# Reordering the steps of the two middle blocks of a convolution and recurrence mixer: input preparation moved to their second part, key and router copies ahead of modulation

## The reference

```python
h = rms_norm(x, g_pre_mix[l]) * (1.0 + sc1) + sh1
proj = h @ w_in[l]
cv, cg, q, f, i, g = jnp.split(proj, IN_SPLITS, axis=-1)
y_conv = conv_module(cv, cg, dw_kernel[l], dw_bias[l], conv_ln_gain[l], conv_ln_bias[l])
y_rec = hgrn2(q, f, i, g, lb_table[l], rec_norm_gain[l])
y = jnp.concatenate([y_conv, y_rec], axis=-1) @ w_out[l]
x = x + gt1 * rms_norm(y, g_post_mix[l])
h = rms_norm(x, g_pre_ffn[l]) * (1.0 + sc2) + sh2
```

## Time and profile before

| | |
|---|---|
| median of three runs | 1663.68 us |
| the profiled execution | 1662.17 us, its span 1660.4 us |
| TensorE busy | 1520.1 us, 92% of the span, granted clock 0.954 on average |
| VectorE, ScalarE, GpSimd busy | 1210.6, 876.0, 367.1 us |
| steps of block 1 | 436.5 to 547.5 us |
| steps of block 2 | 678.0 to 787.4 us |

### The profile page before, as it was taken

How to read it: one execution, slowest core, us unless ns; L and a number is a source line. 1 busy time by engine, 2 the same in 40 slices (tenths; PEclk the granted TensorE clock), 3 DMA queues, 4 the chain that set the end, 5 groups by cost and what they waited for, 6 DMA issues and landing times. The chain is left out here.

```text
span 1660.4 us, 23932 instructions
## 1 busy us (share of the span) xinstructions
PE 1520.1 (92%) x7453; PEld 1106.6 (67%) x7455; DVE 1210.6 (73%) x1932; ACT 876.0 (53%) x1534; POOL 367.1 (22%) x396
## 2 busy tenths in 40 slices
PE   4899879999989999999999999658999999999974
PEld 2779754889755889666889565445676677766741
DVE  2587994597975598974698945576788878777837
ACT  3324362324574324563324533356788887878846
POOL 1000000000010000011000011123476667665640
PEclk8899979999999999999999998769999999999996
DMA  9452361332332323332321543469999998889859
GB/s 320 168 185 94 93 260 42 89 102 78 126 102 76 102 79 100 116 113 77 89 89 52 228 127 114 153 228 329 352 295 274 344 262 240 223 243 284 275 109 384
DMA packets 201445, 291.27 MB, mean 175 GB/s; under 512 B 10558, under 2 KB 158171, under 8 KB 201370
## 3 DMA queue, kind: packets, MB, share of 16 engines
q1 hardware_dynamic: 171840, 197.18, 34.8%
q0 software_dynamic: 29360, 92.99, 20.5%
q10 hardware_dynamic: 170, 0.10, 0.0%
HBM read 240.42 MB, written 59.26 MB: 180 GB/s over the span
## 5 line engine op out<-in xcount | busy, mean ns | idle before, releaser
L1038 DVE SCALAR_TENSOR_TENSOR cv<-late_rows,taps,cv 128x512 f32<-128x512 f32 x480 | 321.8, 746 | 0.0
L1962 DVE TENSOR_TENSOR w_rest<-wgu,w_high 128x1024 fp32r<-128x1024 f32 x192 | 233.8, 1221 | 88.9 <-ACT w_high L1885 85.5
L1885 ACT ACTIVATE w_high<-wgu 128x1024 fp32r x192 | 201.7, 1054 | 97.9 <-PE pgu L1830 75.9
L531 PE MATMUL bank<-wo,yT 128*128 128x512 f32 x512 | 226.5, 599 | 3.6 <-ACT hT L736 2.5
L488 PE MATMUL bank<-hT_high,tiles_operand 128*128 128x512 f32 x496 | 197.2, 398 | 1.1 <-DVE logits L1132 1.1
L489 PE MATMUL bank<-hT_operand,tiles_operand 128*128 128x512 f32 x496 | 196.6, 396 | 0.0
L490 PE MATMUL bank<-hT_high,win_operand 128*128 128x512 f32 x496 | 196.6, 396 | 0.0
L531 PEld LDWEIGHTS bank<-wo,yT 128*128 128x128 f32 x512 | 96.7, 192 | 119.7 <-issue 117.7
L1840 PE MATMUL py<-wd,hTe 128*128 x384 | 172.7, 592 | 1.8 <-DVE hTe L1985 0.9
L1828 PE MATMUL pgu<-w_high,x_high 128*128 128x512 f32 x384 | 156.8, 408 | 3.8 <-DVE x_rest L1977 3.8
L1016 DVE TENSOR_TENSOR win_operand<-win,tiles_operand 128x2048 fp32r<-128x2048 f32 x48 | 109.9, 2290 | 58.1 <-ACT tiles_operand L758 58.0
(11 more groups left out here) (389 smaller groups left out, 2846.7 us busy)
## 6 DMA issues: line engine op xcount, KB each, us to landing
win<-w_in_in SPq DMA_DIRECT2D x64, 512.0 KB, 5.2
wgu<-w_gate_in SPq DMA_DIRECT2D x32, 1024.0 KB
wgu<-w_up_in SPq DMA_DIRECT2D x32, 1024.0 KB
wd<-w_down_in SPq DMA_DIRECT2D x32, 1024.0 KB
win<-w_in_in SPq DMA_DIRECT2D x16, 1024.0 KB, 5.1
wo<-w_ada_in POOLq DMA_DIRECT2D x6, 2048.0 KB, 11.2
y_dram<-zeros POOLq DMA_DIRECT2D x17, 512.0 KB, 5.1
tiles<-x_in POOLq DMA_DIRECT2D x16, 512.0 KB, 6.0
```

What stands on the lines that cost most here:

```text
L531: last = nc.tensor.matmul(out[:], yT[:, w % 2, k, :], wo[:, k, half * 512:(half + 1) * 512], start=(k == 0), stop=(k == KD - 1))
L1038: ins = V.scalar_tensor_tensor(out=cv[:, j], in0=u[:, j, w:w + T], scalar=tap, in1=cv[:, j], op0=ALU.mult, op1=ALU.add)
L1885: A(w_high[:, QK * q:QK * q + QK, :], c.wgu[:, bass.ds(slot, 1), QK * q:QK * q + QK, :].rearrange("p a k n -> p (a k) n"), ACT.Copy).then_ ...
L1962: V.tensor_tensor(w_rest[:, part, :], c.wgu[:, bass.ds(slot, 1), part, :].rearrange("p a k n -> p (a k) n"), w_high[:, part, :].bitcast(F3 ...
```

## The change

The `MIDDLE` lists of TensorE, ScalarE and VectorE are written in a new order. Preparing the next block's input (`T`, `xsum`, `xnorm`, `raw`) leaves the first part of the steps: `T` 0 comes behind `O` 1, `T` 3 behind `B` 3. `y` 1 1 is cut in two halves of four matmuls, around `B` 0. On ScalarE `key`, `turned` of tile 1, `rin` of tile 0 and others stand where `high` and `raw` were; `gate` comes behind `x1sum` 0. On VectorE `scale` comes behind `mask` 0. At the end TensorE does `r` 2, `oT` 2, `r` 3 ahead of `l` 2 and `piece` 0. `T` of odd tiles takes banks 0 and 1. The square in `x_sums` writes its unused output to `hT` instead of `ob`, so `osave` of tiles 0 and 1 no longer waits for the next input's sums, and `modulate` waits for them.

```diff
@@ bank_of
-                return 2 * (1 if i == 3 else i) + half if t < 0 else 2 + half
+                return 2 * (1 if i == 3 else i) + half if t < 0 else 2 + half if t == 0 or i % 2 == 0 else half
@@ y_half
-            def y_half(t, w, half):
-                if half == 0:
+            def y_half(t, w, half, part=None):
+                first, final = part in (None, 0), part in (None, 1)
+                if half == 0 and first:
...
-                out = take("y", w, half, t)
-                for k in range(KD):
+                out = take("y", w, half, t) if first else place("y", w, half, t)
+                for k in range(0 if first else KD // 2, KD if final else KD // 2):
...
-                last.then_inc(y_ready, 1)
+                if final:
+                    last.then_inc(y_ready, 1)
@@ TensorE, MIDDLE
-            MIDDLE = [("y", 0, 0), ("T", 0), ("mean",), ("T", 1), ("y", 0, 1), ("T", 2), ("var",), ("T", 3), ("y", 1, 0),
+            MIDDLE = [("y", 0, 0), ("mean",), ("y", 0, 1), ("var",), ("y", 1, 0), ("A", 0), ("y", 1, 1, 0), ("B", 0),
...
@@ x_sums
-                if i == 0:
-                    wait(act, oT_psum, (t - 1) * NT)
-                ch.link(A(ob[:].rearrange("p a n -> p (a n)"), xt_of(t, i), ACT.Square, accum_out=sums[:, i:i + 1]))
+                ch.link(A(hT[:, :, i * P:(i + 1) * P], xt_of(t, i).rearrange("p (k n) -> p k n", k=KD), ACT.Square,
+                          accum_out=sums[:, i:i + 1]))
@@ modulate
+                dve.wait_ge(x_rstd, t * NT + i + 1)
@@ save_outputs
-                elif t < NB - 1:
-                    dve.wait_ge(x_rstd, (t + 2) * NT)
                 else:
-                    dve.wait_ge(oT_psum, t * NT)
+                    wait(dve, oT_psum, t * NT)
```

More of the change, by code:

```diff
@@ L915, in _ @@
                      ("turned", 3)]
[L916 to L923, removed]
+            MIDDLE = [("ln", 0), ("ln", 1), ("ln", 2), ("end", 0), ("exps", 0), ("sq", 0), ("sq", 1), ("sq", 2),
+                      ("sq", 3), ("exps", 1), ("end", 1), ("ln", 3), ("exps", 2), ("end", 2), ("var",), ("ysum", 0),
+                      ("exps", 3), ("end", 3), ("xsum", 0), ("key", 0), ("x1sum", 0), ("gate",), ("xsum", 1),
+                      ("ysum", 1), ("key", 1), ("rin", 0), ("osq", 0), ("orstd", 0), ("x1sum", 1), ("key", 2),
+                      ("raw", 0), ("turned", 0), ("osq", 1), ("rin", 1), ("raw", 1), ("orstd", 1), ("xsum", 2),
+                      ("turned", 1), ("high", 0), ("high", 1), ("split", 0), ("raw", 2), ("ysum", 2), ("x1sum", 2),
+                      ("osq", 2), ("xsum", 3), ("orstd", 2), ("high", 2), ("key", 3), ("ysum", 3), ("raw", 3),
+                      ("high", 3), ("x1sum", 3), ("rin", 2), ("osq", 3), ("rin", 3), ("orstd", 3), ("turned", 2),
+                      ("split", 1), ("turned", 3)]
             FINAL = [("ln", 0), ("ln", 1), ("ln", 2), ("end", 0), ("exps", 0), ("sq", 0), ("sq", 1), ("sq", 2), ("sq", 3),
@@ L1204, in _ @@
                      ("gateo", 2), ("oms", 3), ("gateo", 3), ("rest", 1), ("logit", 3)]
[L1205 to L1215, removed]
@@ new lines, in _ @@
+            MIDDLE = [("scan", 0), ("diff", 0), ("centre",), ("head", 0), ("scan", 1), ("diff", 1), ("scan", 2),
+                      ("head", 1), ("diff", 2), ("scan", 3), ("head", 2), ("diff", 3), ("head", 3), ("ynorm", 0),
+                      ("mask", 0), ("scale",), ("state", 0, 0), ("x1norm", 0), ("xnorm", 0), ("state", 0, 1),
+                      ("ynorm", 1), ("mask", 1), ("osave", 0), ("xnorm", 1), ("state", 1, 0), ("oms", 0),
+                      ("gateo", 0), ("place", 0), ("state", 1, 1), ("logit", 0), ("osave", 1), ("mask", 2),
+                      ("raw", 0), ("x1norm", 1), ("state", 2, 0), ("oms", 1), ("gateo", 1), ("raw", 1), ("place", 1),
+                      ("logit", 1), ("xnorm", 2), ("input", 0), ("state", 2, 1), ("osave", 2), ("raw", 2),
+                      ("input", 1), ("ynorm", 2), ("rest", 0), ("oms", 2), ("x1norm", 2), ("gateo", 2), ("input", 2),
+                      ("xnorm", 3), ("mask", 3), ("place", 2), ("state", 3, 0), ("raw", 3), ("ynorm", 3),
+                      ("osave", 3), ("state", 3, 1), ("input", 3), ("x1norm", 3), ("oms", 3), ("logit", 2),
+                      ("gateo", 3), ("logit", 3), ("place", 3), ("rest", 1)]
```

## The result

The changed kernel takes 1678.24 us (median of 4 runs, 1675.88 to 1680.62), the kernel before in the same comparison 1663.13 (4 runs, 1662.35 to 1665.45): a ratio of 1.0091, 95% interval 1.0075 to 1.0108. It is slower, as forecast, but by 15.1 us where 1671 meant 7.3, and 1678 lies outside the range of 1665 to 1677. The profiled execution, the slowest of the four, took 1680.62 us (span 1678.9) against 1662.17 (span 1660.4): 18.5 more.

A forecast was written before the change was run, and what follows sets the result against it. TensorE was taken to bound the middle blocks. Front -0.1 and end +3.8 make 3.7 us a block, 7.4 for two, on 1662.17: 1669.6, or 1671 as the runs' median; range 1665 to 1677.

The forecast's parts named there:

- The waits: Middle blocks: TensorE's new waits less those gone, front -0.1 and end +3.8, 3.7 us a block, 7.4 for two.
- The front comes out even: Up to y(2,0): gaps at y(1,0), B(0), O(0) gone, -3.65 us a block; new waits at O(1), B(2), +3.55.
- What was put at nothing: Middle blocks: later loads taken as 0 (0 to 1 us a block); square's new destination and lost output wait cost nothing.
- The clock: TensorE's granted clock in the middle blocks, as gaps go and come: from -1.6 us in all to +1.6 a block.
- rival 4: The clock falls in both middle blocks' new gaps: 1.6 to 3.2 us more, 1672 to 1675 by the runs; chance 0.15.
- Rival 3: Gate's two table loads each hold ScalarE 1.4 us longer, O(1) 2.8 later: 1675.2 (1677 by the runs); chance 0.03.
- Rivals 1 and 2: Middle blocks: gaps close without successors, 1656 by the runs, chance 0.05; or front gains, end still costs 3.8, 1663.5, 0.12.

The follow-up runs named there:

- E2: The changed kernel with dummy transposes in three TensorE gaps of each middle block, ahead of O(1), oT(2) and r(3): 1665.60 us, ratio 1.0023.
- E6: The kernel before, order untouched, with dummy transposes in some TensorE gaps of all four blocks: 1656.32 us, ratio 0.9968.
- E3: The changed kernel with ScalarE's sum of tile 1 and raw(0) and VectorE's xnorm(1) moved later at the middle blocks' front: 1673.62 us, ratio 1.0077.
- E5: The changed kernel with the old order at the middle blocks' end and the queue moves at their front together: 1660.64 us, ratio 0.9992.
- E4: The kernel before with only the order at the end of the middle blocks changed as in the change: 1673.86 us, ratio 1.0079.
- E1: The changed kernel with the old order at the middle blocks' end, T(3) kept ahead, ScalarE and VectorE queues reordered to suit: 1669.47 us, ratio 1.0037.

## Why the prediction was wrong in size

The ledger of the two middle blocks, from one execution each. E2 has the waits of the changed kernel with no fall of the clock, E6 those of the kernel before, also with none:

| | both blocks, us |
|---|---|
| before, no fall (E6) | 479.77 |
| waits: E2 less E6 | +7.03 |
| clock: after less E2 | +10.98 |
| clock: before less E6 | 1.59, to be taken off |
| after less before | 7.03 + 10.98 - 1.59 = 16.42 |

Block 2 of both, up to `y(2,0)` and over all steps, E2 first, then E6:

```profile
680.95:740.75 59.80, 56.38 (x295) 34.42 (x294) 45.78 (x88) 41.20 (x93) 6.61 (x10) 1.00 0.32 105
680.95:793.85 112.90, 108.31 (x563) 68.13 (x561) 74.94 (x147) 67.03 (x154) 11.08 (x16) 1.00 0.32 103
...
679.41:741.05 61.64, 57.86 (x308) 35.97 (x307) 50.89 (x101) 48.05 (x108) 6.62 (x10) 1.00 0.40 126
679.41:788.81 109.40, 104.97 (x533) 65.14 (x531) 74.72 (x147) 66.33 (x153) 11.10 (x16) 1.00 0.34 106
```

- **The waits: right.** Forecast 3.7 a block, 7.4 in all; measured 7.03. With the clock held up the steps take 112.90, where the forecast said about 113. Right in its parts too: gaps at y(1,0), B(0) and O(0) gone, A(0) on time, O(1), B(2), oT(2) and r(3) late by the amounts worked out.
- **"The front comes out even": right, for the waits.** At `y(2,0)` E2 is at 59.80, E6 at 61.64 with two more T (1.8) done by then: even within 0.1. The end then costs 3.5, forecast 3.8. O(1) starts 47.79 us into block 2, before 52.32 with four T (3.5) ahead of it: 1.0 ahead, forecast 0.9. E3 shows why: ysum(1) behind gate and sum of tile 1, and xnorm(1) ahead of the state update.
- **What was put at nothing** (loads, square, lost wait): right by E5.
- **The step that failed is "The clock".** The sum has nothing for it; as an unknown it was allowed from -1.6 in all to +1.6 a block, the size of block 1's surplus in the earlier trace rows, and rival 4 gave the fall in both blocks 0.15. It fell twice in each, and the term measures 9.4 net. The fall at the front was of the size allowed: up to `y(2,0)` the changed kernel needs 61.44 in block 2, 1.6 more than E2. The end is what was mis-sized, 4.0 there. The 1.6 of the earlier trace rows came from O(0)'s surroundings, a fall of some 3 us in work that half waits; at the end of the block TensorE was at 1.2 GHz from 788.5 to 798.5, through r(3), l(2) and the first matmuls of piece 0, 8.5 us busy in 10: E4 puts that at 4.1. The forecast had both gaps there in its sum, side by side, 3.85 us of them, and did not ask what they do to the clock and to the dense work behind.
- **Rival 4** was thus the mechanism, with a price (1.6 to 3.2) at most a third of the 9.4. **Rival 3** (dearer table loads) is out: the silu starts at 720.01, 0.01 behind the load's end at 720.00, and ScalarE passes through gate and loads in 5.5 us as before. **Rivals 1 and 2** are out by the timeline.
- The runs of one kernel spread by some 10 us, the slower ones at a lower mean clock (E1: 1669.97 at 0.948, 1660.51 at 0.958). That this is also why medians and block sums differ is likely, but not shown.

## What to carry to other kernels

Price a gap of TensorE twice: its idle time, and, where the clock falls, half the busy time that follows at the lower clock (half of 8.5 is 4.3; E4 has 4.1). Gaps of 1 to 2.5 us that stand close together, ahead of dense work, cost more by the second than by the first where it fell (4.1 against 3.0 at the end of this block). When an order is moved, keep the long unit (a y half, a projection piece) between a chain's start and its waiter; if a wait can't be covered, harmless matmuls into a free bank keep the clock up: E2's median is 2.7 above the kernel before, the changed kernel's 15.1.

## What the hardware showed that was not expected

- The granted clock falls with TensorE working most of the time: in E3 it fell in block 1 right behind three gaps of 0.75, 0.78 and 0.87 us, the longest around, and not in block 2 behind the same three. At the end of the block it fell in one block of E4 and not in the other, behind nearly the same waits. So a single profile doesn't tell what a gap costs. The Trainium skill (TensorE: Matmul & The Clock Gate, "What's actually happening") says that the throttled state is the default and activity releases it; E2 agrees: with transposes of no use in the gaps the clock stayed at 1.00 in both blocks.
- The lower clock outlasts the gaps in front of it: after the wait for oT(2) the engine was busy for 8.54 of 10.00 us and still stood at 0.50.
- Forty extra transposes a block in the gaps delay no real work: O(1) starts 47.73 us into block 1 with them, 47.78 without.
